# A decoder step on one Trainium2 core: where two latent norms are applied in the MLA projections, and where the decode latent queries are computed

## The reference, cut to what matters

```
def mla_project(x, pos, w_down, g_q, w_uq, g_kv):
    d = x @ w_down
    c_q = rmsnorm(d[..., :384], g_q)
    c_kv = rmsnorm(d[..., 384:640], g_kv)
    k_pe = rope(d[..., 640:], pos)
    q = (c_q @ w_uq).reshape(B, S, 8, 128 + 64)
    return q[..., :128], rope(q[..., 128:], pos), c_kv, k_pe
# prompt: k_nope = c_kv @ w_uk, v = c_kv @ w_uv, causal softmax over 4 blocks of 128 queries
# decode: q_lat = einsum('bthd,rhd->bthr', q_nope, w_uk), scores against the cached latents
def rmsnorm(x, g):
    return x * rsqrt(mean(x * x, -1) + 1e-6) * g
```

## Time and profile before

| what | value |
|---|---|
| median of the runs | 2543.24 us |
| profiled execution, its own time | 2541.57 us |
| its span, first to last instruction | 2539.9 us |
| mean granted TensorE clock | 0.982 |
| busy in the span: PE, DVE, ACT, POOL | 97%, 40%, 31%, 34% |

### The profile page before, as it was taken

The page is one execution under the profiler, slowest core; times in us unless marked ns, Lnnn a source line. Parts: engine busy times, 40 slices in busy tenths (PEclk is TensorE's granted clock), DMA queues, the critical chain, the costliest instruction groups (busy, mean ns, idle before and its releaser), DMA issues.

```text
span 2539.9 us, 43955 instructions
## 1 busy us (share of the span) xinstructions
PE 2456.1 (97%) x17572; PEld 2311.0 (91%) x17572; DVE 1021.0 (40%) x1935; ACT 790.2 (31%) x1392; POOL 852.8 (34%) x477
## 2 busy tenths in 40 slices
PE   8999999899899999999999999999999999999997
PEld 8999999785455999999999999999988889999997
DVE  5222213576432553222244332225477666323223
ACT  5222223313333342222234222224322344222221
POOL 3333332120231233333323333331367422333332
PEclk9999999998999999999999999999999999999999
DMA  3222222130461222222222222221211332222222
GB/s 122 84 83 83 79 85 87 49 106 9 121 192 45 67 67 84 83 83 85 79 70 83 84 83 83 84 84 59 84 59 50 116 110 67 84 83 83 78 85 75
DMA packets 68648, 209.04 MB, mean 82 GB/s; under 512 B 8380, under 2 KB 21181, under 8 KB 68254
## 3 DMA queue, kind: packets, MB, share of 16 engines
q1 hardware_dynamic: 65438, 196.58, 25.1%
q0 software_dynamic: 3072, 10.49, 1.4%
HBM read 199.22 MB, written 7.82 MB: 82 GB/s over the span
## 4 chain that ended last, share of the span: by engine, by line
PE 89%; DVE 7%; ACT 1%; POOL 1%; issue 1%; DMA 1%; POOLq 0%; SPq 0%; DVEq 0%
PE psum L1537 25%; PE psum L1539 25%; PE psum L1538 25%; PE psum L1822 1%; PE psum L1838 1%; DVE h L1010 1%; PE psum L1894 1%; PE psum L1773 1%; DVE y_ffn L1006 1%; PE psum L1976 1%; DVE x_lo L980 1%; DVE work L1001 1%; PE psum L1772 1%; PE psum L1780 1%; DVE w_lo L989 1%
## 5 line engine op out<-in xcount | busy, mean ns | idle before, releaser
L869 POOL TENSOR_TENSOR w_lo<-raw,w_hi 128x1024 fp32r<-128x1024 f32 (+2 forms) x315 | 735.2, 2336 | 1439.3 <-ACT w_hi L520 1439.3
L1537 PE MATMUL psum<-x_hi,w_hi 128*128 128x288 f32 x3568 | 1074.7, 301 | 21.6 <-DVE x_lo L980 17.7
L1539 PE MATMUL psum<-x_hi,w_lo 128*128 128x288 f32 x3568 | 1055.0, 296 | 0.0
L1538 PE MATMUL psum<-x_lo,w_hi 128*128 128x288 f32 x3568 | 1054.1, 295 | 0.0
L1537 PEld LDWEIGHTS psum<-x_hi,w_hi 128*128 128x128 f32 x3568 | 673.1, 189 | 39.2 <-DVE x_lo L980 27.3
L1538 PEld LDWEIGHTS psum<-x_lo,w_hi 128*128 128x128 f32 x3568 | 673.0, 189 | 3.9
L1539 PEld LDWEIGHTS psum<-x_hi,w_lo 128*128 128x128 f32 x3568 | 672.6, 189 | 0.0
L520 ACT ACTIVATE w_hi<-raw 128x1024 fp32r<-128x1024 f32 (+2 forms) x331 | 341.5, 1033 | 813.7 <-DMA raw<-ffn_in 362.3
L1026 DVE TENSOR_TENSOR work<-psum,r_pre 128x288 f32<-128x288 f32 x352 | 160.1, 457 | 662.2 <-PE psum L1539 661.7
L1537 PE MATMUL psum<-gu_hi,w_hi 128*128 128x288 f32 x1408 | 415.5, 295 | 0.0
L1539 PE MATMUL psum<-gu_hi,w_lo 128*128 128x288 f32 x1408 | 414.7, 295 | 0.0
(11 more groups left out here) (262 smaller groups left out, 1950.9 us busy)
## 6 DMA issues: line engine op xcount, KB each, us to landing
raw<-ffn_in SPq DMA_DIRECT2D x176, 512.0 KB, 3.6
raw<-ffn_out SPq DMA_DIRECT2D x64, 448.0 KB, 3.3
raw<-ffn_out SPq DMA_DIRECT2D x32, 512.0 KB, 3.5
raw<-gla_in SPq DMA_DIRECT2D x25, 512.0 KB, 3.6
cache<-cache SPq DMA_DIRECT2D x64, 160.0 KB, 2.9
cache<-cache POOLq DMA_DIRECT2D x64, 160.0 KB, 3.1
raw<-mla_wo SPq DMA_DIRECT2D x8, 512.0 KB, 3.6
raw<-gla_wo SPq DMA_DIRECT2D x8, 512.0 KB, 3.6
```

The source lines that it names most:

```text
L869: pool.tensor_tensor(w_lo[slot][:, 0:w], raw[slot][:, 0:w], w_hi[slot][:, 0:w].bitcast(F32), ALU.subtract).then_inc(s_lo, 1)
L1537: pe.matmul(out, wh, xh, start=start, stop=False)
L1538: pe.matmul(out, wh, xl, start=False, stop=False)
L1539: return pe.matmul(out, wl, xh, start=False, stop=stop)
```

## The change

It makes three moves.

1. Query norm. The split operands `cq_hi` and `cq_lo` are made from `down` times the gain alone. The factor `r_q` is applied when the up-projection's product is evicted: `qn` is multiplied by `r_q` instead of copied, and `rope_tab` is multiplied by `r_q` once, so that the rotation applies it.
2. Key norm. Its square sums (`M_KV`), roots, reciprocals and the latent product come behind the second query head, and `ckv_s` and `kv_lo` behind the fourth.
3. Latent queries of decode. Head by head they are computed behind the eight value units, into banks 6 and 7 in the layout that is wanted, and evicted by two copies of 512 columns. The first two `scores` wait for their own bank alone, the third and fourth for everything; `q_pes` is copied ahead of the key units.

The diff, cut to its core, in the order ScalarE, VectorE, TensorE:

```diff
+                act.wait_ge(s_mg, 2)
+                for j in range(QT):
+                    act.activation(cq_hi[:, j, :], down[:, j, :], ACT.Identity,
+                                   scale=mla_g[:, j:j + 1]).then_inc(s_cqhi, 1)
+                for dst, eps, u in ((r_q, eps_q, u0 + M_SUM), (r_kv, eps_kv, u0 + M_KV)):
                     for hf in range(2):
...
-                for j in range(QT):
-                    act.wait_ge(s_cq, j + 1)
-                    act.activation(cq_hi[:, j, :], down[:, j, :], ACT.Copy).then_inc(s_cqhi, 1)
                 for j in range(KT):
                     act.wait_ge(s_ckv, j + 1)
                     act.activation(kv_hi[:, j, :], ckv[:, j, :], ACT.Copy).then_inc(s_kvhi, 1)
...
-                for j in range(QT):
-                    dve.scalar_tensor_tensor(out=down[:, j, :], in0=down[:, j, :], scalar=mla_g[:, j:j + 1],
-                                             in1=r_q[:, :], op0=ALU.mult, op1=ALU.mult).then_inc(s_cq, 1)
...
                 for j in range(QT):
                     dve.wait_ge(s_cqhi, j + 1)
+                    dve.scalar_tensor_tensor(out=cq_lo[:, j, :], in0=down[:, j, :], scalar=mla_g[:, j:j + 1],
+                                             in1=cq_hi[:, j, :].bitcast(F32), op0=ALU.mult,
+                                             op1=ALU.subtract).then_inc(s_cqlo, 1)
+                for hf in range(2):
+                    dve.wait_ge(s_mroot, hf + 1)
+                    dve.reciprocal(r_q[:, H[hf]], r_q[:, H[hf]]).then_inc(s_evicted, 1)
+                dve.tensor_tensor(rope_tab[:, :], rope_tab[:, :], r_q[:, :], ALU.mult).then_inc(s_cq, 1)
...
                 for hd in range(HEADS):
+                    u = u0 + q_unit(hd)
+                    if hd == 2:
+                        latent()
+                    if hd == 4:
+                        latent_low()
                     for hf in range(2):
                         dve.wait_ge(s_unit, u + hf + 1)
-                        dve.tensor_copy(qn[:, hd, H[hf]], bank[(u + hf) % RING][:, 0:HALF]).then_inc(s_evicted, 1)
+                        dve.tensor_tensor(qn[:, hd, H[hf]], bank[(u + hf) % RING][:, 0:HALF], r_q[:, H[hf]],
+                                          ALU.mult).then_inc(s_evicted, 1)
...
-                    for hd in range(HEADS):
-                        last = dve.tensor_copy(q_lat[:, rt, :, hd * DEC_SEQ:(hd + 1) * DEC_SEQ],
-                                               bank[u % RING][:, hd * NEW:(hd + 1) * NEW].rearrange(
-                                                   "p (b t) -> p b t", t=DEC_SEQ))
-                    last.then_inc(s_evicted, 1)
+                    dve.tensor_copy(q_lat[:, rt, :, :].rearrange("p b q -> p (b q)"), bank[6 + rt]).then_inc(s_evicted, 1)
...
+                square_sums(0, QT, u0 + M_SUM)
                 pe.wait_ge(s_cqlo, QT)
                 for hd in range(HEADS):
                     n = n0 + MLA_IN + hd
+                    if hd == 2:
+                        square_sums(QT, QT + KT, u0 + M_KV)
...
+                        hd = QB * b + t
+                        for rt in range(KT):
+                            out = bank[6 + rt].rearrange("p (b q) -> p b q", q=QR)[:, :, hd * DEC_SEQ:(hd + 1) * DEC_SEQ]
+                            last = pe.matmul(out, uk_t[:, hd, rt * P:(rt + 1) * P],
+                                             qn[:, hd, SEQ:TOK].rearrange("p (b t) -> p b t", t=DEC_SEQ), start=True, stop=True)
...
+                bank_free(S_BANK[0])
                 scores(0)
+                bank_free(S_BANK[1])
                 scores(1)
+                pe.wait_ge(s_evicted, u0 + M_O)
+                scores(2)
+                scores(3)
                 for w in range(ATT):
-                    if w + 2 < ATT:
+                    if LOOK <= w + 2 < ATT:
                         scores(w + 2)
```

More of the change, by code:

```diff
@@ L1159, in mla @@
-                for j in range(KT):
-                    dve.scalar_tensor_tensor(out=ckv[:, j, :], in0=down[:, QT + j, :], scalar=mla_g[:, QT + j:QT + j + 1],
-                                             in1=r_kv[:, :], op0=ALU.mult, op1=ALU.mult).then_inc(s_ckv, 1)
-                dve.wait_ge(s_ckv, KT)
-                dve.tensor_copy(ckv_s[:, :, :], ckv[:, :, SEQ:TOK]).then_inc(s_ckvs, 1)
                 for j in range(QT):
                     dve.wait_ge(s_cqhi, j + 1)
-                    dve.tensor_tensor(cq_lo[:, j, :], down[:, j, :], cq_hi[:, j, :].bitcast(F32),
-                                      ALU.subtract).then_inc(s_cqlo, 1)
@@ L1168, in mla @@
-                for j in range(KT):
-                    dve.wait_ge(s_kvhi, j + 1)
-                    dve.tensor_tensor(kv_lo[:, j, :], ckv[:, j, :], kv_hi[:, j, :].bitcast(F32),
-                                      ALU.subtract).then_inc(s_kvlo, 1)
+                    dve.scalar_tensor_tensor(out=cq_lo[:, j, :], in0=down[:, j, :], scalar=mla_g[:, j:j + 1],
+                                             in1=cq_hi[:, j, :].bitcast(F32), op0=ALU.mult,
+                                             op1=ALU.subtract).then_inc(s_cqlo, 1)
@@ L1173, in mla, with latent_low @@
+                def latent_low():
+                    dve.wait_ge(s_ckv, KT)
+                    dve.tensor_copy(ckv_s[:, :, :], ckv[:, :, SEQ:TOK]).then_inc(s_ckvs, 1)
+                    for j in range(KT):
+                        dve.wait_ge(s_kvhi, j + 1)
+                        dve.tensor_tensor(kv_lo[:, j, :], ckv[:, j, :], kv_hi[:, j, :].bitcast(F32),
+                                          ALU.subtract).then_inc(s_kvlo, 1)
                 r = 0
                 for hd in range(HEADS):
-                    u = u0 + M_Q + 4 * hd
+                    u = u0 + q_unit(hd)
[3 more added lines that the diff above has]
+                        latent_low()
@@ L1192, in mla @@
                         r += 1
+                dve.wait_ge(s_rope, 2 * HEADS)
+                for hd in range(HEADS):
+                    dve.tensor_copy(q_pes[:, :, hd * DEC_SEQ:(hd + 1) * DEC_SEQ],
+                                    qpe[:, hd, SEQ:TOK].rearrange("p (b t) -> p b t", t=DEC_SEQ)).then_inc(s_qpes, 1)
                 for hd in range(HEADS):
@@ L1727, in mla @@
                         for hf in range(2):
-                            u = u0 + M_Q + 4 * hd + 2 * part + hf
+                            u = u0 + q_unit(hd) + 2 * part + hf
                             free(u)
@@ L1753, in mla, with bank_free @@
                         last.then_inc(s_unit, 1)
[L1755 to L1764 removed]
+                        hd = QB * b + t
[3 more added lines that the diff above has]
+                                             qn[:, hd, SEQ:TOK].rearrange("p (b t) -> p b t", t=DEC_SEQ), start=True, stop=True)
+                            if hd == HEADS - 1:
+                                last.then_inc(s_unit, 1)
+                def bank_free(bk):
+                    pe.wait_ge(s_evicted, max(u for u in range(u0 + M_V, u0 + M_L) if u % RING == bk) + 1)
                 def scores(w):
```

58 lines of the change are left out of this document (25 added, 33 removed).

## The result

| kernel | median, us | range (runs) | ratio to before, 95% |
|---|---|---|---|
| before | 2543.32 | 2540.88 to 2543.8 (4) | |
| changed | 2521.89 | 2515.44 to 2522.96 (4) | 0.9914 [0.9899, 0.9929] |
| changed, a second session | 2522.09 | 2517.23 to 2525.73 (6) | 0.9923 [0.9905, 0.9941] |

The forecast was 2526.4, with a range of 2521 to 2533. The change wins 21.4 us where 16.9 were forecast. The median lies 0.9 us inside that range.

A forecast was written before the change was run, and what follows sets the result against it. TensorE, 89% of the chain, was taken as the bound. 10.5 us by the latents' end (12.5 in the first gap, less 2 of stall) plus 6.4 in the second made 16.9: 2524.7, plus 1.67 gives median 2526.4, range 2521 to 2533.

The forecast's parts named there:

- The first gap: Before the query heads: 12.3 us of waiting and 2.1 of slow start won, less 1.9 for key norm sums: 12.5 us.
- What is late next: In the query heads: VectorE lags, so TensorE waits about 2 us, mostly in heads 6 and 7; ends 0 and 6.
- The latents: Latent queries between value units: 3.7 us as before; ends 0.9 less if weight loads hide, 3.4 more if strided outputs are slow.
- the rival: Latent products' strided PSUM outputs are slow, 0.22 instead of 0.115 us a row: 3.4 us, time 2529.8; chance 0.07.
- The second gap: Latents' end to first head_out's end: 22.95 us becomes 16.5 if the clock stays (2 to 1), 6.4 won; otherwise 1.4.
- The clock did not fall in the first head: Rival at the attention's first head: the clock falls to 0.50 again, 11.9 us won, time 2531.3; chance 0.25.
- VectorE did not become the bound: Rival in the query heads: VectorE bounds them, 6 us of waits instead of 2, time 2530.4; chance 0.12.
- At the cache pages nothing was given back: Rival behind the attention: all that is won is waited for at the cache pages' loads, time 2543; chance 0.03.
- two sentences of the sum: Whole kernel: 10.5 + 6.4 = 16.9 us won, 2524.7 for the profiled execution, 2526.4 for the median; chance 0.50.
- the forecast's own range: Whole kernel: 2522.5 to 2529, from ends of 0 and 4 us of stall and the latents' 0.9.
- The case of a gain over 21 us: Whole kernel: no stall, hidden weight loads and another piece of clock give over 21 us; chance 0.01.
- the weight loads did not hide: At the latents: weight loads might hide in the value units, making the latents 0.9 us less than 3.7.

The follow-up runs named there:

- contiguous kernel: Changed kernel, but each latent product writes 64 adjoining columns of its bank and VectorE's copies rearrange them: 2520.26 us, ratio 0.992.
- the matmuls ahead of the attention: Kernel before with five more matmuls, results unread, between the latents and the wait ahead of the attention: 2531.61 us, ratio 0.996.
- the later start: Changed kernel, but all four first scores wait until everything is evicted, as before the change: 2521.53 us, ratio 0.9934.
- moves 1 and 2 alone: Kernel before with the query norm and key norm moves, latent queries and start of the attention as before: 2533.41 us, ratio 0.9963.
- two variants of the changed kernel: Changed kernel with the key norm ahead of the first head again, 2519.14 us; changed kernel with 28 unused matmuls at the cache pages, 2523.12 us.
- the version with the early squares: Changed kernel, with four squares and cq_hi ahead of two weight splits, and cq_lo ahead of the last down tile's evictions: 2510.8 us, ratio 0.9884.

## Why the prediction was right, and where it was short

- *The first gap* (12.5 won, less 2 of stall). From the last down product to the first key unit 12.0 and 10.9 us were won, against 10.5. The first up-projection starts 0.4 us ahead of the modelled end of the sums, not behind `cq_lo`; the sums took 5.27 instead of 5.99 us, as the clock rose earlier in them. The wait for ScalarE's squares ahead of them, which the prediction left as it was, stayed (5.65 us).
- *What is late next.* VectorE, as forecast, by 1.0 and 3.0 us (2 taken, bounds 0 and 6). In the second session's profile they fell at 530.06 and 540.77, in the sixth and the eighth head (heads 6 and 7 were named), and one of 1.1 us at the keys, where none was forecast: the last sum of the heads took 2.48 us beside a split there. The `q_pes` copies, priced at 0.9 us, took that in the second profile. In the first they took 3.1 us, one of the eight 2.39 us of it, while GpSimd's split, 546.09 + 2.41, ran beside them (timeline of the changed kernel below); TensorE did not wait for it in that profile.

```profile
545.64 3.11 DVE L1213 COPY q_pes<-qpe 64x64 f32<-64x64 f32 x8
...
546.09 2.41 POOL L875 TENSOR_TENSOR w_lo<-raw,w_hi 128x1024 fp32r<-128x1024 f32 x1 [2.32 <-ACT w_hi L526]
```

- *The latents* (3.7, ends 2.8 and 7.1). Value units with a latent pair are 1.83 us apart, 0.47 over a value unit alone. No stride cost; the rival falls by the contiguous kernel.
- *The second gap* (6.4). Measured 7.0 from 22.95 to 16.0, and the clock stayed at 1.00. The prediction split this into 1.4 us of order and waiting and 5 of clock, and the matmuls ahead of the attention show the clock's share, 5.5. The reason given for its staying was half right: the dense value units between the latents go with it, the shortness of the wait is not needed, as the later start showed.
- *The rivals.* The clock did not fall in the first head; it does with moves 1 and 2 alone, where it stays low for 24 us, so the worry was real. VectorE did not become the bound. At the cache pages nothing was given back in one profile and 1.5 us in the other.
- *Where the forecast was short.* The stage gave 18.4 and 16.4 us where 16.9 were forecast, so what is missing on the median, 4.5 us, lies in two sentences of the sum. One is "Everything behind the attention is TensorE's chain and shifts with it": it shifts, but it does not always run the same. Between the profiles 7.0 and 3.9 us were won at the decode value product and behind it, by the clock. Since that product also ran at the low clock in two variants of the changed kernel, this is no sure effect of the change. The other is "The median of the runs lies 1.67 above that execution", which takes the clock of the profiled execution for that of the median one. In another execution of the same code the first head took 27.8 us, not 22.95, and the changed kernel saves those 4.9 too. Either is large enough; the share of each in the median was not measured. The profiled execution had the cheaper first head and the dearer value product, and so came out near the median by chance.
- *The chances.* The median is 0.6 us below the forecast's own range of 2522.5 to 2529 and inside the stated one. The case of a gain over 21 us had 0.01, too little: it is what came, 21.4 and 21.1. Of its reasons, the stall did not vanish (1.0 and 3.0 us) and the weight loads did not hide (0.47 us for a pair of latent products, 0.46 forecast); "another piece of clock" is the one that fits.

## What to carry to other kernels

A factor that belongs to the other axis of a product can go behind the product: here it took a wait of 10.36 us for VectorE out of TensorE's way and cost nothing at the eviction. Small products that run in a row next to a wait are worth moving between dense ones, for the clock more than for the time that they take. When a stage moves earlier, look at the granted clock at every later short wait before saying that the rest shifts unchanged. And one profile shows one execution: where the clock is low in it, ask for a second one before comparing with a median.

## What the runs showed that was not expected

- Added matmuls made the kernel before faster: 11.5 us with five ahead of the attention, 4.9 with seven at the value product.
- A wait of 1.23 us behind a row of small products was followed by 20 us and more at 1.2 GHz with TensorE busy all the time, while a wait of 1.59 us behind dense products cost no clock. What separates the two beyond the products ahead of the wait was not tried.
- The 54 runs of before lie 17 us apart (2531.4 to 2548.4), the five of the version with the early squares 3 us apart (2509.87 to 2513.03). The pieces at half clock differ between executions of one program: 13.7 or some 24 us in the first head. From the value product on it is none to 13.7 us over the kernels profiled. The runs of that version are too few to say that it has fewer kinds.
- Copies on VectorE from SBUF to SBUF get longer beside GpSimd's splits too: eight `q_pes` copies of 64 columns took 3.11 us beside a split, and 0.9 without one in the second profile of the changed kernel.
